# Half of the MLP's second product by seven block products instead of eight

## The reference

```python
def sq_relu_mlp(h, w1, w2):
    a = jax.nn.relu(h @ w1)
    return (a * a) @ w2
...
MLP_HIDDEN = 4 * D_MODEL
...
        x = x + sq_relu_mlp(rms_norm(x, norm_mlp[layer]), mlp_w1[layer], mlp_w2[layer])
```

## Time and profile before

| | |
|---|---|
| median of 3 runs | 2127.73 us (2127.24 to 2127.94) |
| the profiled execution | 2128.13 us, its span 2125.8 us |
| PE busy (matmuls, modelled ends) | 2117.1 us, 100% |
| DVE busy | 1413.6 us, 66% |
| ACT busy | 1060.2 us, 50% |
| POOL (GpSimd) busy | 39.8 us, 2% |
| DMA: SP's queue | 52.4% of 16 engines' span, 397.95 MB |
| granted TensorE clock | 1.000 |

### The profile page before, as it was taken

The page is one execution under the profiler, slowest core; times in us unless marked ns, Lnnn a source line. Parts: engine busy times, 40 slices in busy tenths (PEclk is TensorE's granted clock), DMA queues, the critical chain, the costliest instruction groups (busy, mean ns, idle before and its releaser), DMA issues.

```text
span 2125.8 us, 27295 instructions
## 1 busy us (share of the span) xinstructions
PE 2117.1 (100%) x10836; PEld 1781.8 (84%) x10836; DVE 1413.6 (66%) x1938; ACT 1060.2 (50%) x1316; POOL 39.8 (2%) x28
## 2 busy tenths in 40 slices
PE   9999999999999999999999999999999999999999
PEld 7878888888887888888888888888888888888887
DVE  7888878778778867765675566556546555655653
ACT  6665565455564555663555545444334434433432
POOL 0000000000000000000010011000000000000000
PEclk9999999999999999999999999999999999999999
DMA  8555555455544744445564554455555455555553
GB/s 309 200 215 182 198 192 184 182 195 181 196 178 158 238 164 151 147 160 197 196 213 171 191 182 167 159 181 194 184 195 197 181 195 198 181 196 198 181 205 129
DMA packets 62701, 399.68 MB, mean 188 GB/s; under 512 B 7088, under 2 KB 9840, under 8 KB 16112
## 3 DMA queue, kind: packets, MB, share of 16 engines
q1 hardware_dynamic: 62576, 397.95, 52.4%
HBM read 395.75 MB, written 2.16 MB: 187 GB/s over the span
## 4 chain that ended last, share of the span: by engine, by line
PE 94%; DVE 1%; ACT 0%; issue 0%; POOL 0%; DVEq 0%
PE bank L898 20%; PE bank L900 19%; PE bank L899 19%; PE bank L878 19%; PE bank L882 10%; PE bank L960 1%; PE bank L1108 1%; PE bank L1044 1%; PE bank L1066 0%; PE bank L1003 0%; PE bank L1096 0%; PE bank L973 0%; PE bank L1121 0%; PE bank L946 0%; PE bank L1077 0%
## 5 line engine op out<-in xcount | busy, mean ns | idle before, releaser
L1578 DVE TENSOR_TENSOR wlo<-raw,whi 128x2048 fp32r<-128x2048 f32 x353 | 808.2, 2290 | 433.5 <-ACT whi L1172 404.7
L1172 ACT ACTIVATE whi<-raw 128x2048 fp32r<-128x2048 f32 x353 | 675.4, 1913 | 449.7 <-PE bank L900 445.3
L878 PE MATMUL bank<-A,whi 128*128 128x512 f32 x2000 | 479.6, 392 | 0.0
L878 PEld LDWEIGHTS bank<-A,whi 128*128 128x128 f32 x2000 | 367.8, 188 | 72.9 <-issue 1.2
L898 PE MATMUL bank<-whi,A2h 128*128 128x512 f32 x1024 | 401.2, 392 | 0.0
L900 PE MATMUL bank<-wlo,A2h 128*128 128x512 f32 x1024 | 398.8, 389 | 0.0
L899 PE MATMUL bank<-whi,A2l 128*128 128x512 f32 x1024 | 398.6, 389 | 0.0
L898 PE MATMUL bank<-whi,A 128*128 128x512 f32 x832 | 330.4, 397 | 2.9 <-DVE wlo L1566 1.2
L900 PE MATMUL bank<-wlo,A 128*128 128x512 f32 x832 | 324.3, 390 | 0.0
L899 PE MATMUL bank<-whi,A 128*128 128x512 f32 x832 | 324.2, 390 | 0.0
L882 PEld LDWEIGHTS bank<-A,wlo 128*128 128x128 f32 x2000 | 256.4, 191 | 9.7
(11 more groups left out here) (222 smaller groups left out, 1316.6 us busy)
## 6 DMA issues: line engine op xcount, KB each, us to landing
raw<-wst SPq DMA_DIRECT2D x353, 1024.0 KB, 4.8
W<-cum_scratch SPq DMA_DIRECT2D x8, 1024.0 KB, 6.9
W<-rows SPq DMA_DIRECT2D x21, 256.0 KB, 6.0
raw<-wst SPq DMA_DIRECT2D x16, 256.0 KB, 7.3
W<-nabias SPq DMA_DIRECT2D x16, 160.0 KB, 4.0
XR<-xtok SPq DMA_DIRECT2D x2, 1024.0 KB, 9.2
out<-XR SPq DMA_DIRECT2D x8, 256.0 KB, 2.2
W<-xT SPq DMA_DIRECT2D x3, 512.0 KB, 7.8
```

What stands on the lines that cost most here:

```text
L878: e.matmul(o[:, :], whi[:, s, k * P:(k + 1) * P], A1[:, k, :, :].rearrange("p h t -> p (h t)"), start=k == 0, stop=False)
L1172: e.activation(whi[:, u % 3, :], raw[:, u % 3, :], ACT.Copy).then_inc(*hi.inc((u, 3)))
L1578: e.tensor_tensor(wlo[:, u % 3, :], raw[:, u % 3, :], whi[:, u % 3, :], ALU.subtract).then_inc(*lo.inc((u, 3)))
```

## The change

The lower half of a hidden quarter (tiles 8 to 15) times two neighbouring column blocks of `w2` is a product of 2 x 2 blocks: X11, X12 are the first 128 tokens of hidden tiles 8 to 11 and 12 to 15, X21, X22 the other 128 tokens; B11, B12 are the left and right column block of tiles 8 to 11, B21, B22 of tiles 12 to 15. Each Bij is one unit of 1 MB. Before, four units with two halves each made eight block products of 12 matmuls. Now it is seven, of a new form P, one bank and 12 matmuls each (`product_block`), named a to g:

| | activations | weights | how the weights come about |
|---|---|---|---|
| a | X11 | B11 | loaded into a buffer of its own (the chain) |
| c | X21-X22-X11+X12 | B22 | loaded |
| b | X21-X22 | B11+B12 | GpSimd issues a DMA that adds B12 to the chain (`acc`) |
| d | X21-X22-X11 | B11+B12+B22 | DVE adds c's buffer to the chain (`add`) |
| e | X12 | B21 | loaded |
| f | X11-X21 | B12+B22 | GpSimd issues a DMA that adds B12 to c's buffer |
| g | X22 | B11+B12+B21+B22 | DVE adds e's buffer to the chain |

That is done for both pairs of column blocks (p = 0 and 1) in quarters 0 to 2 and for the left pair in quarter 3: seven times, and called **a seven** below. The upper half (tiles 0 to 7) stays in form B, two units a block in place of four.

What comes with it:

- **Order.** The seven units of form P alternate with others, `-a-c-b-d-e-f-g`, where each dash is another unit: B units of the same quarter for p = 0, A units of the next quarter's `up` for p = 1. The list has 378 units in place of 357. Seven P units take the place of four B units, each time.
- **Mixing of activations** (`mixed`), once a quarter, behind the split that is issued in the step of the first unit after `("up", s, 15)`: four DVE operations of 128 x 512 elements, three ACT copies and three DVE subtractions (1024, 512 and 512 columns). The squared tiles 8 to 15 are now written to a place of their own for it (`hidden`).
- **Emptying** (`drain`). c, e and g go on in the bank of the B units of their block. a is copied to SBUF by ACT (`kept`). b, d and f have a bank each, and their sums go to two or three pieces of the residual: per seven 11 DVE operations of 128 x 512 on P units (b 2, c 1, d 3, e 1, f 3, g 1), and 1 after the B units. Before, the same two blocks had 4.
- **Buffers.** A fourth raw buffer and two chains are laid in W, the work space that the MLP leaves free. The load of a unit waits for the split (and the add) of the one that held its buffer. All eight PSUM banks serve both forms in the MLP.

```diff
+M_MIX, M_RING, M_CHAIN = 0, 2048, 7168
...
+def products(s, p):
...
+    top, low = 16 * s + 8, 16 * s + 12
+    left, right = 1024 * p, 1024 * p + 512
+    return {"a": (top, left), "b": (top, right), "c": (low, right), "d": None, "e": (low, left), "f": (top, right),
+            "g": None}
+def in_turn(order, first, others):
+    first, others = iter(first), iter(others)
+    return [next(others if c == "-" else first) for c in order] + [*others]
...
+    u += b(("upb",), "mlp_w1_2", 0)
...
+    def down(s, nbs):
+        return [("B", ("down", s, nb, i), "mlp_w2_2", 16 * s + 4 * i, nb * 512) for nb in nbs
+                for i in range(2 if seven(s, nb) else 4)]
...
+    def sevens(s, p):
+        return [("P", ("dp", s, p, name), "mlp_w2_2", *(at or (None, None))) for name, at in
+                ((x, products(s, p)[x]) for x in "acbdefg")]
...
     for s in range(QT):
-        first = 4 if s == 0 else 0
-        if first:
-            u += b(("upb",), "mlp_w1_2", 0)
-        u += [("A", ("up", s, i), "mlp_w1_2", (16 * s + i) * P) for i in range(first, 16)]
-        u += [("B", ("down", s, nb, i), "mlp_w2_2", 16 * s + 4 * i, nb * 512) for nb in range(ND) for i in range(4)]
+        ups = [("A", ("up", s, i), "mlp_w1_2", (16 * s + i) * P) for i in range(0 if s else 4, 16)]
+        u += in_turn("-a-c-b-d-e-f-g", sevens(s - 1, 1), ups) if s else ups
+        u += in_turn("-a-c-b-d-e-f-g", sevens(s, 0), down(s, (1, 0, 2, 3)))
...
+def seven(s, nb):
+    return s < QT - 1 or nb < 2
...
+    for s in range(QT):
+        after[at["up", s, 15] + 1].append(("mix", s))
...
+def sums(units, u):
+    def name(n):
+        return units[n][1][3] if n < len(units) and units[n][0] == "P" else None
+    def unit(n, x):
+        return next(m for m, v in enumerate(units) if v[1] == units[n][1][:3] + (x,))
+    if name(u + 2) == "a":
+        yield ("acc", unit(u + 2, "b"))
+    if name(u + 3) in ("d", "g"):
+        yield ("add", u + 3)
+    if name(u + 3) == "d":
+        yield ("acc", unit(u + 3, "f"))
...
+def shut(tag):
+    if tag[0] == "down" and seven(tag[1], tag[2]):
+        return (1,) if tag[2] % 2 and tag[3] == 1 else ()
+    return (0, 1) if tag[0] == "ao" or tag[-1] == 3 else ()
...
+def drains(tag):
...
+    left, right = 2 * tag[2], 2 * tag[2] + 1
+    return {"a": (), "b": ((1, right, 1), (0, right, 1)), "c": ((0, right, 1),),
+            "d": ((0, left, 1), None, (0, right, -1)), "e": ((0, left, 1),), "f": (None, (1, right, -1), (1, left, 1)),
+            "g": ((1, left, 1),)}[tag[3]]
...
             def load(u):
-                if u < NU:
-                    w.wait_ge(*hi((u - 3, 3)))
-                    w.wait_ge(*lo((u - 3, 3)))
-                    e.dma_start(raw[:, u % 3, :], wst[u]).then_inc(s_raw[u % 3], 16)
+                if u < NU and u in FREED:
+                    before = FREED[u]
+                    if before is not None:
+                        name = units[before][1][3] if units[before][0] == "P" else None
+                        split = last_read(before) if name in ("a", "c") else before
+                        w.wait_ge(*hi((split, 3)))
+                        w.wait_ge(*lo((split, 3)))
+                        if name == "e":
+                            w.wait_ge(*add_v(product(before, "g")))
+                    elif RAW[u] >= MLP_ONLY:
+                        w.wait_ge(*x3_v("l1", ND - 1))
+                    e.dma_start(raw_of(u), wst[tile_at[u]]).then_inc(s_raw[RAW[u]], 16)
...
+            def product_block(u, o):
+                s, p, name = units[u][1][1:]
+                weights_ready(u, 3)
+                for k in range(4):
+                    h, low, ready = factor(s, name, k)
+                    for made in ready:
+                        w.wait_ge(*made)
+                    wh, wl = (x[:, u % 3, k * 512:(k + 1) * 512] for x in (whi, wlo))
+                    e.matmul(o, h, wh, start=name in ("a", "b", "d", "f") and k == 0, stop=False)
+                    e.matmul(o, low, wh, start=False, stop=False)
+                    last = e.matmul(o, h, wl, start=False, stop=k == 3)
+                last.then_inc(*mm.inc((u, 0)))
+            def factor(s, name, k):
+                if name in "aeg":
+                    i, t = (8 if name == "a" else 12) + k, int(name == "g")
+                    c = slice(t * P, (t + 1) * P)
+                    return A2h[:, i, c], A2l[:, i, c], (up_a("h", at["up", s, i]), up_v("l", at["up", s, i]))
+                if name == "b":
+                    h, low = ((A2h[:, 8 + k, P:T], A2l[:, 8 + k, P:T]) if s < QT - 1 else
+                              (A1h[:, k, 0:P], A1l[:, k, 0:P]))
+                else:
+                    i = 1024 + k * P if name == "c" else k * T + (0 if name == "d" else P)
+                    h, low = mixr[:, 0, i:i + P], mixr[:, 1, i:i + P]
+                return h, low, (mix_a("h2", s), mix_v("l2", s))
...
+            def mixed(s):
+                w.wait_ge(*mix_v("4", s))
+                for n, (high, _, x) in enumerate(parts_of(s)):
+                    e.activation(high, x, ACT.Copy).then_inc(*mix_a.inc(f"h{n}", s))
...
+            def add(u):
+                name = units[u][1][3]
+                other = product(u, "c" if name == "d" else "e")
+                before = product(u, "b" if name == "d" else "d")
+                w.wait_ge(*hi((before, 3)))
+                w.wait_ge(*lo((before, 3)))
+                w.wait_ge(*raw_in(other))
+                e.tensor_tensor(raw_of(u), raw_of(u), raw_of(other), ALU.add).then_inc(*add_v.inc(u))
+            def mixed(s):
+                for i in range(8, 16):
+                    w.wait_ge(*up_v("l", at["up", s, i]))
+                a = mix.rearrange("p (q k t c) -> p q k t c", q=2, k=4, t=NT)
+                a11, a21, a12, a22 = (a[:, q, :, t, :] for q in range(2) for t in range(NT))
+                for to, x, y, op, name, before in ((a22, a21, a22, ALU.subtract, "1", None),
+                                                   (a21, a11, a21, ALU.subtract, "3", "1"),
+                                                   (a11, a22, a11, ALU.subtract, "2", "3"),
+                                                   (a12, a11, a12, ALU.add, "4", "2")):
+                    if before:
+                        w.wait_ge(*mix_v(before, s))
+                    e.tensor_tensor(to, x, y, op).then_inc(*mix_v.inc(name, s))
+                w.wait_ge(*mix_v("4", s))
+                for n, (high, low, x) in enumerate(parts_of(s)):
+                    w.wait_ge(*mix_a(f"h{n}", s))
+                    e.tensor_tensor(low, x, high, ALU.subtract).then_inc(*mix_v.inc(f"l{n}", s))
+            def drain(u, n):
+                form, tag = units[u][:2]
+                ps = bank[BANK[u, n if form == "B" else 0]][:, :]
+                w.wait_ge(*(mm_done(u) if form == "P" else mm((u, n))))
+                if not DRAINS[u, n]:
+                    w.wait_ge(*(evac_v((u, 0)) if tag[3] == "d" else evac_v((product(u, "d"), 2))))
+                    e.tensor_tensor(kept(u), ps, kept(u), ALU.add).then_inc(*evac_v.inc((u, n)))
+                    return
+                t, nb, sign = DRAINS[u, n]
+                x, r = xr(t, nb), (S_R2SQ if sign > 0 else S_NSQ) + t
+                if form == "P" and tag[3] in ("d", "f"):
+                    ps = kept(u)
+                    w.wait_ge(*(evac_v((u, n - 1)) if n else keep_a(product(u, "a"))))
+                w.wait_ge(*(evac_v(PIECE[u, n]) if PIECE[u, n] else residual_ready(t, nb, "down")))
+                w.wait_ge(*rms_v("nsq", 1))
+                mul_add(x, ps, SM[:, r:r + 1], x, ALU.mult, ALU.add).then_inc(*evac_v.inc((u, n)))
...
+                if form == "P":
+                    for n in range(len(drains(tag))):
+                        drain(u, n)
+                    return
...
+            def acc(u):
+                before = product(u, "a" if units[u][1][3] == "b" else "c")
+                w.wait_ge(*hi((before, 3)))
+                w.wait_ge(*lo((before, 3)))
+                if units[u][1][3] == "f":
+                    w.wait_ge(*add_v(product(u, "d")))
+                e.dma_start(raw_of(u), wst[tile_at[u]], accum_op=ALU.add).then_inc(s_acc[RAW[u]], 16)
...
-    nc = _bacc.Bacc("TRN2", target_bir_lowering=False, num_devices=1)
+    nc = _bacc.Bacc("TRN2", target_bir_lowering=False, num_devices=1, dynamic_dma_scratch_size=4096)
```

More of the change, by code:

```diff
@@ L42 @@
 QUANT = 12288.0
+RING = 4
+MLP_ONLY = 3
 ALU = mybir.AluOpType
@@ L223, in script @@
             yield ("lo", u + 2)
+        yield from sums(units, u)
         if u == 6:
@@ L365, in stack_kernel @@
         hi, lo = Marks(sem("hi_done"), split_order("hi")), Marks(sem("lo_done"), split_order("lo"))
+        add_v = Marks(sem("weights_added"), [s[1] for s in SCRIPT if s[0] == "add"])
         mm = Marks(sem("mm_done"), [(s[1], s[2]) for s in SCRIPT if s[0] == "mm" and s[3][-1] in (3, KT - 1)])
         def mm_done(u):
```

(53 more changed lines are left out.)

146 lines of the change are left out of this document (117 added, 29 removed).

## The result

| | before | after |
|---|---|---|
| median | 2127.54 us (2127.24 to 2127.94, 4 runs) | 2112.86 us (2112.64 to 2112.99, 4 runs) |
| span of the profiled execution | 2125.8 us | 2110.9 us |
| TensorE instructions | 10836 | 10752 |

A forecast was written before the change was run, and what follows sets the result against it. TensorE was taken as the bound, busy 2117.1 of 2125.8 us. The sum 2128.13 - 19.0 + 3.6 + 0.9 = 2113.6 us for the profiled execution was said as 2113.0 for the median, range 2108 to 2130.

The forecast's parts named there:

- What goes: TensorE in the MLP: seven times 12 matmuls leave the path, 84 x 0.2267 = 19.0 us.
- The walk through the mixing: After each quarter's last `up`: TensorE waits 0.9 us at c for its split; four times, 3.6 us.
- Load of VectorE: DVE's work per seven: 53.8 of 58.0 us with A units (93%), 51.1 of 57.1 with B units (89%).
- ACT's 33.4: ACT's work in a seven with A units: 33.4 of 58 us, so ACT isn't short.
- The 0.3 us for each A seven: Allowance for DVE's lag using up the slack at the end of each of three sevens with A units.
- step 8: Of 14 steps in a seven with A units: starts 13.86 us after step 5 starts, split done at 18.8.
- The 0.9 us: Sum of the 0.3 us put on each of the three sevens with A units.
- VectorE as the bound: Rival in the sevens: 0.07 us more per DVE operation costs 11.6 us, so 2125; chance 0.14.
- The adding DMA: Two GpSimd DMAs per seven, for b and f: landing taken as 10 us, between 4.8 and 20; 10 is hidden.
- The rival's mechanism: Late adding DMA at `whi` of b and f: each us beyond some 18 paid 14 times, 2141 at 20; chance 0.20.
- The port rule: GpSimd, writing descriptors for its DMAs, can be shut out while VectorE holds their shared port pair; no size given.
- Quarters 1 and 2: Sign that the forecast is right: these quarters take about 176.1 - 5.4 + 1.2 = 172 us.

The follow-up runs named there:

- the four-sevens kernel: The changed kernel with seven block products only for the left pair of column blocks, eight for the right, none beside A units: 2121.36 us.
- the kernel without stops: The changed kernel with ACT's three mixing copies and DVE's three mixing subtractions one step later, behind the split of c: 2109.08 us.
- the run with 2.54 us: The changed kernel with three more, unused DVE operations of 128 x 640 behind the addition for g in each seven: 2113.2 us.

## Why the prediction was right, and where not

- **What goes**: right. 84 matmuls fewer at 0.227 us, 19.0 us; the four-sevens kernel prices three of the seven alone, at 8.5 (7.3 to 9.0) where 36 matmuls are 8.2.
- **The walk through the mixing**: right in time and cause. On the walk's clock `whi` of c was to be done at 12.1, `wlo` at 14.5, with a wait of 0.9; measured from 1507.1 they are done at 11.8 and 14.2, and TensorE waits 0.82. Moving the copies took 3.8 us back, where the term was 3.6 (now 3.3 of stops and 0.4 behind them), and the kernel without stops takes 2109.1, where the prediction has 2108.7 if nothing waits.
- **Load of VectorE**: the counts were right, the share nearly. The rows of an A seven's window, with the one split and the one hidden tile that fall outside it, add up to 53.5 us (forecast 53.8), those of a B seven to 51.3 (51.1). The windows show 82% and 83% busy where 93% and 89% were forecast, for two reasons. In the A window 3.6 us of the seven's work come behind its end, in the B window 2.1 of the last split. And rows overlap, by 2.2 and 1.6 us, which busy time doesn't count twice; the earlier trace rows showed that, and the prediction named it without taking it off. With both taken into account DVE has 51.3 us for 58.0 (89%) and 49.7 for 57.2 (87%). ACT's 33.4 is a slip: its terms add up to 32.9.
- **The 0.3 us for each A seven: the step that failed**, though the sum hides it. The walk holds from step 8 on, to within 0.2 us: from the start of step 5 (1587.1) `wlo` 15 is done 41.41 us on, forecast 41.3, and TensorE comes to the unit at 41.49, forecast 41.45. In steps 5 to 7 it runs 0.7 to 1.0 us early, since it starts with DVE free where DVE was still at the split of step 4; the slack there hides it. Wrong was what it says of every unit, that the split "must be done when TensorE comes to n+2". It is so for B and P units, not for an A unit, whose first reader of `wlo` starts 3.63 us later. And it took the slack at the end for all the slack, where DVE also stands idle 1.26 us behind the addition for g. No A seven has a stop. The 0.9 us was right by luck: in its place stand 0.1 us of the A sevens, 0.4 behind the four stops and 0.4 in the rest of the B sevens, which no term foresaw.
- **VectorE as the bound**: its price was worked out from the same 0.1 us, so it would have come far too early: at 0.07 us an operation, 2.5 us a seven, where the run with 2.54 us shows nothing. With the load behind the addition for g it binds between 2.5 and 5.1 us more a seven.
- **The adding DMA**: 10 us taken, 8.2 and 8.0 measured, inside the bounds; twice a plain one in the engines' time, as assumed. Hidden, with the window of 18 us confirmed from both sides: one that lands some 15.5 us after the issue of the change costs nothing, one that lands some 28 us after it costs 9.7 in the first seven, which puts the edge at some 18. The rival's mechanism is real for b (f wasn't tried); its price lacked the 1.6 to 2.3 us of slower matmuls behind a long stop. By its own 14 us for each us beyond 18, the gain of 14.7 would be gone at 19.1, not at 19.4.
- **The port rule** of the Trainium skill ("SBUF — State Buffer", section "Who interferes with whom") is not one that speaks against these DMAs. It lets VectorE lock GpSimd out of writing descriptors in VectorE's 2-port modes, and says of `tensor_tensor` that it has none and that a probe did not show it stalling DMAs. The splits and the additions here are TENSOR_TENSOR rows (of SCALAR_TENSOR_TENSOR, the emptyings, it says nothing), and the trace agrees: with VectorE 82% busy no issue took over 1.05 us (median 0.87) and no landing over 9.6.
- **Quarters 1 and 2**: 172 us forecast; c starts at 1521.38, 1693.11 and 1864.85, so 171.7 each.

## What to carry to other kernels

When work is taken off the bounding engine, walk the order of the others through one period, and for each tile write down which half of it is read when: the deadline is the instruction that reads it, not the unit's start. Where an engine waits for a neighbour with work queued behind that needs nothing of it, put that work ahead of the wait; here that one move was worth a quarter of the change's gain. Price a stop of TensorE with what follows it: short ones (0.8 us) cost 0.1 more, long ones (6 to 10 us) 1.6 to 2.3.

## What the runs showed of the hardware

- A 1 MB DMA that adds into SBUF lands 8.0 to 8.2 us after its issue in the median (10.2 and 10.3 in the runs that issue the one for b later), a plain one on the same queue 5.1; it takes the 16 DMA engines twice the time.
- After 6 to 10 us without matmuls, the first seven to eleven start 0.43 us apart, at a granted clock of 0.50 to 0.51, then 0.23 at 1.00.
- A stop of 0.8 us leaves the clock at 1.00; only the first spacing is longer, 0.31 us.
